# Tokens ordered by grid column, with branch B's softmax, copies and values cut to the 160 keys that a tile can see, in a two-layer encoder

## What is computed

```python
A  = differential attention (4 heads, T5 relative bias)
B  = 2-D neighbourhood attention on the 64-wide token grid (8 heads, own 2-D bias)
C  = dilated sliding-window attention (8 heads, T5 relative bias)
x += (sum_i sigmoid(g_i) * (branch_i @ W_br_i)) @ W_o
```

```python
kh = min(NA_ROWS_MAX, rows)          # 4, so every row
kw = min(NA_COLS, GRID_W)            # 16
cstart = jnp.clip(col - kw // 2, 0, GRID_W - kw)
cidx = cstart[:, None] + jnp.arange(kw)[None, :]
s = jnp.einsum('bhqd,bhrqcd->bhqrc', qrow, knb) + bias
pr = jax.nn.softmax(s.reshape(B, B_HEADS, GRID_W, kh * kw), axis=-1)
return jnp.einsum('bhqrc,bhrqcd->bhqd', pr, vnb)
```

## Time and profile before

| | |
|---|---|
| runs (us) | 1266.9, 1267.26, 1269.08 |
| profiled execution (us) | 1267.46 |
| its span, first to last instruction (us) | 1265.4 |
| granted TensorE clock, mean | 0.998 |
| TensorE matmul busy | 1255.7 us, 99% |
| VectorE busy | 842.6 us, 67% |
| ScalarE busy | 679.2 us, 54% |
| GpSimd busy | 39.0 us, 3% |
| DMA | 245.05 MB, mean 194 GB/s |

### The profile page before, as it was taken

The page is one execution under the profiler, slowest core; times in us unless marked ns, Lnnn a source line. Parts: engine busy times, 40 slices in busy tenths (PEclk is TensorE's granted clock), DMA queues, the critical chain, the costliest instruction groups (busy, mean ns, idle before and its releaser), DMA issues.

```text
span 1265.4 us, 17533 instructions
## 1 busy us (share of the span) xinstructions
PE 1255.7 (99%) x6763; PEld 1067.9 (84%) x6763; DVE 842.6 (67%) x1196; ACT 679.2 (54%) x920; POOL 39.0 (3%) x55
## 2 busy tenths in 40 slices
PE   9999999999999999999999999999999999999997
PEld 6888888888878888888888888888888788888886
DVE  6576667557767766556675666766577777655665
ACT  7454555546866354454554445554477543644544
POOL 0311100000000000000000000000000000000000
PEclk9999999999999999999999999999999999999999
DMA  8697855565644545555445555455556454555551
GB/s 281 233 288 233 262 215 200 199 213 187 238 124 148 190 171 195 199 188 182 178 184 199 199 183 185 163 204 201 194 203 214 122 192 169 188 194 199 199 192 40
DMA packets 59211, 245.05 MB, mean 194 GB/s; under 512 B 21344, under 2 KB 27616, under 8 KB 32408
## 3 DMA queue, kind: packets, MB, share of 16 engines
q1 hardware_dynamic: 58144, 242.54, 55.1%
q10 hardware_dynamic: 984, 1.80, 0.4%
q0 software_dynamic: 32, 0.02, 0.0%
HBM read 239.07 MB, written 5.27 MB: 193 GB/s over the span
## 4 chain that ended last, share of the span: by engine, by line
PE 97%; DVE 2%; issue 0%; DMA 0%; ACT 0%; POOL 0%; POOLq 0%; SPq 0%; DVEq 0%; ACTq 0%
PE bank L796 30%; PE bank L800 16%; PE bank L763 16%; PE bank L765 15%; PE bank L764 15%; PE bank L1117 1%; PE bank L1094 1%; PE bank L849 1%; PE bank L856 1%; PE bank L1108 1%; DMA params<-in_params 0%; DVE wlo L1227 0%; DVE nat L1483 0%; DVE qkT L1434 0%; DVE nat L1479 0%
## 5 line engine op out<-in xcount | busy, mean ns | idle before, releaser
L1227 DVE TENSOR_TENSOR wlo<-raw,whi 128x2048 fp32r<-128x2048 f32 x209 | 479.3, 2296 | 302.6 <-ACT whi L467 296.1
L467 ACT ACTIVATE whi<-raw 128x2048 fp32r<-128x2048 f32 x206 | 393.0, 1911 | 233.8 <-PE bank L800 143.5
L796 PE MATMUL bank<-xT,whi 128*128 128x512 f32 x1664 | 395.3, 390 | 0.0
L796 PEld LDWEIGHTS bank<-xT,whi 128*128 128x128 f32 x1664 | 308.7, 188 | 61.7
L800 PEld LDWEIGHTS bank<-xT,wlo 128*128 128x128 f32 x1664 | 207.1, 192 | 4.8 <-issue 0.5
L800 PE MATMUL bank<-xT,wlo 128*128 128x256 f32 x1664 | 209.2, 283 | 0.0
L763 PE MATMUL bank<-whi,xT 128*128 128x512 f32 x432 | 171.9, 398 | 1.0 <-DVE qkT L1434 1.0
L765 PE MATMUL bank<-whi,xT 128*128 128x512 f32 x432 | 168.5, 390 | 0.0
L764 PE MATMUL bank<-wlo,xT 128*128 128x512 f32 x432 | 168.3, 390 | 0.0
L763 PE MATMUL bank<-whi,hTh 128*128 128x512 f32 x320 | 124.5, 389 | 0.0
L764 PE MATMUL bank<-wlo,hTh 128*128 128x512 f32 x320 | 124.5, 389 | 0.0
(11 more groups left out here) (182 smaller groups left out, 1054.9 us busy)
## 6 DMA issues: line engine op xcount, KB each, us to landing
raw<-in_stream SPq DMA_DIRECT2D x209, 1024.0 KB, 4.8
bias<-t_rows SPq DMA_DIRECT2D x24, 256.0 KB, 8.2
bias<-in_rpb SPq DMA_DIRECT2D x16, 256.0 KB, 7.8
masked<-bias SPq DMA_DIRECT2D x8, 512.0 KB, 6.8
bias<-masked SPq DMA_DIRECT2D x8, 512.0 KB, 6.6
raw<-in_stream SPq DMA_DIRECT2D x10, 256.0 KB, 6.5
x<-in_x SPq DMA_DIRECT2D x4, 256.0 KB, 5.6
raw<-in_stream ACTq DMA_DIRECT2D x2, 256.0 KB, 4.4
```

Of the source, the lines that this page charges most:

```text
L467: act.activation(whi[:, s, :], raw[:, s, :], ACT.Copy).then_inc(hi_ready, 1)
L796: return pe.matmul(dst[blk][:, :], whi[:, s, w], xT[:, 4 * a + k, :, :].rearrange("p a s -> p (a s)"), start=start, stop=stop)
L1227: dve.tensor_tensor(wlo[:, s, :], raw[:, s, :], whi[:, s, :].bitcast(F32), ALU.subtract).then_inc(unit_split, 1)
```

## The change

Tokens lie by grid column: partition p of tile t holds grid column 32 t + p // 4 and grid row p % 4. x is loaded and the output stored through a rearranged view of DRAM (`rows_by_cols`). A tile of 32 columns sees at most 40 columns, so of the 256 keys it sees 160: keys 0 to 159 for tile 0 and 96 to 255 for tile 1 (`seen`). For branch B the bias step, the exponentials, the normalisation, the copy of the turned probabilities and the value matmuls work on those 160; the other 96 probabilities are filled with zeros before the turn, which is still in full width, as are the scores. The biases stay in order of position within a row of keys, and the bias step reads them with (column, row) strides, neighbours 64 elements apart (`rearrange("p (r c) -> p c r")`), for all three branches. The masked bias has a row per token, so each is stored in four DMAs of 64 partitions, one per grid row; each bias load of branches A and C becomes one per tile. Last, in VectorE's loop, the first reading of an odd unit's branch product stands ahead of the first due weight split and the second normalisation.

```diff
+COLS = GRID_W // TILES
+SEEN = (COLS + NA_COLS // 2) * GRID_H
+UNSEEN = S - SEEN
...
+        def rows_by_cols(ap, t, c0, c1):
+            return ap[0, :, c0:c1].rearrange("(r c) d -> c r d", r=GRID_H)[t * COLS:(t + 1) * COLS, :, :]
+        def by_cols(ap):
+            return ap.rearrange("p (c r) -> p c r", r=GRID_H)
+        def seen(b, t):
+            return slice(0, S) if b != BB else slice(0, SEEN) if t == 0 else slice(UNSEEN, S)
+        def seen_reversed(b, t):
+            return slice(0, S) if b != BB else slice(UNSEEN, S) if t == 0 else slice(0, SEEN)
...
-                sp.dma_start(masked[j, :, :], bias[:, j % 2, :, :, :].rearrange("p m t k -> p (m t k)")).then_inc(masked_stored, 16)
+                for r in range(GRID_H):
+                    half = slice(r % 2 * GRID_W, (r % 2 + 1) * GRID_W)
+                    sp.dma_start(masked[j, r::GRID_H, :].rearrange("c (m k) -> c m k", m=2), bias[half, j % 2, :, r // 2, :]).then_inc(masked_stored, 16)
...
-                    src = bass.AP(t5_rows.tensor, head * 512, [[1, P], [P, TILES], [1, S]])
-                    sp.dma_start(bias[:, ring, m, :, :], src).then_inc(bias_landed[ring], 16)
+                    for t in range(TILES):
+                        src = bass.AP(t5_rows.tensor, head * 512 + t * COLS, [[1, COLS], [GRID_W, GRID_H], [1, S]])
+                        sp.dma_start(bias[:, ring, m, t, :], src).then_inc(bias_landed[ring], 16)
...
-                        e = act.activation(probs_of(s)[:, m, t, ::-1], sneg_of[s % 2][:, m, t, :], ACT.Exp, scale=-1.0,
+                        p_seen = probs_of(s)[:, m, t, seen(s // 4, t)]
+                        e = act.activation(p_seen[:, ::-1], sneg_of[s % 2][:, m, t, seen_reversed(s // 4, t)], ACT.Exp, scale=-1.0,
...
-                                last = pe.matmul(o_turns(b, blk // 2)[DH * m:DH * m + DH, blk % 2, :], v[:, b, kb, d0:d0 + DH],
-                                                 pT_of[s % 2][:, m, kb, :], start=kb == 0, stop=kb == 1)
+                                asking = seen(b, kb)
+                                last = pe.matmul(o_turns(b, blk // 2)[DH * m:DH * m + DH, blk % 2, asking], v[:, b, kb, d0:d0 + DH],
+                                                 pT_of[s % 2][:, m, kb, asking], start=kb == 0, stop=kb == 1, skip_group_check=b == BB)
...
-                            r = dve.tensor_tensor_reduce(out=sneg_of[ring][:, m, t, :], in0=pair_bank(s, m)[:, t * S:(t + 1) * S],
-                                                         in1=bias[:, ring, 0 if b == BA else m, t, :], scale=-1.0, scalar=3e38,
+                            keys = seen_reversed(b, t)
+                            added = bias[:, ring, 0 if b == BA else m, t, :] if b != BB else bias[:, ring, t, m, :]
+                            r = dve.tensor_tensor_reduce(out=by_cols(sneg_of[ring][:, m, t, keys]),
+                                                         in0=by_cols(pair_bank(s, m)[:, t * S + keys.start:t * S + keys.stop]),
+                                                         in1=added.rearrange("p (r c) -> p c r", r=GRID_H)[:, keys.start // GRID_H:keys.stop // GRID_H, :],
+                                                         scale=-1.0, scalar=3e38,
...
+                        if s // 4 == BB:
+                            dve.memset(pr[:, :, 0, SEEN:S], 0.0)
+                            dve.memset(pr[:, :, 1, 0:UNSEEN], 0.0)
...
                     if j < PAIRS:
                         normalize(j)
+                    _, b, n, _ = MIX[j + 1]
+                    branch_now = MIX[j + 1][0] == "br"
+                    if branch_now:
+                        branch_tile(b, n, U_MIX + j + 1, 0)
                     for w in due[:1]:
                         to_lo(l, w)
                     if j < PAIRS:
                         normalize(j + 1)
                     split_o(j)
-                    _, b, n, _ = MIX[j + 1]
-                    branch_now = MIX[j + 1][0] == "br"
-                    if branch_now:
-                        branch_tile(b, n, U_MIX + j + 1, 0)
```

More of the change, by code:

```diff
@@ L55 @@
 RPB_ROWS, RPB_PITCH = TILES * GRID_H, 128
+COLS = GRID_W // TILES
+SEEN = (COLS + NA_COLS // 2) * GRID_H
+UNSEEN = S - SEEN
+assert NA_ROWS >= GRID_H and COLS * GRID_H == P
 MASK_AT = [6 + 3 * j for j in range(DEPTH * BLK + 1)]
@@ L163, in build @@
         t5_rows = nc.dram_tensor("t5_rows", [T5_HEADS, 512], F32, kind="Internal").ap()
-        masked = nc.dram_tensor("masked", [DEPTH * BLK, P, 2 * TILES * S], F32, kind="Internal").ap()
+        masked = nc.dram_tensor("masked", [DEPTH * BLK, S, 2 * S], F32, kind="Internal").ap()
         t5_high, t5_split, early_mean = map(sem, ("t5_high", "t5_split", "early_mean"))
@@ L240, in n_bias @@
         def n_bias(l, s):
-            per = {BC: 2, BB: 1, BA: 1}
+            per = {BC: 2 * TILES, BB: 1, BA: TILES}
             return 16 * DEPTH * BLK + l * (16 * sum(per[q // 4] for q in range(s % 2, PAIRS, 2))) + 16 * sum(per[q // 4] for q in range(s % 2, s + 1, 2))
@@ L272, in probs_of, with seen_by_keys @@
             return home
+        def rows_by_cols(ap, t, c0, c1):
[6 more added lines that the diff above has]
+            return slice(0, S) if b != BB else slice(UNSEEN, S) if t == 0 else slice(0, SEEN)
+        def seen_by_keys(ap):
+            return bass.AP(ap.tensor, ap.offset, [list(ap.ap[0]), [S + UNSEEN, TILES], [1, SEEN]])
         def pair_bank(s, m):
@@ L300, in load_unmasked @@
                 if j >= 2:
-                    sp.wait_ge(masked_stored, 16 * (j - 1))
+                    sp.wait_ge(masked_stored, 16 * GRID_H * (j - 1))
                 for half in range(2):
@@ L317, in load_bias @@
                 if b == BB:
-                    sp.dma_start(bias[:, ring, :, :, :].rearrange("p m t k -> p (m t k)"), masked[l * BLK + blk, :, :]).then_inc(bias_landed[ring], 16)
+                    sp.dma_start(bias[:, ring, :, :, :].rearrange("p t m k -> p t (m k)"),
+                                 masked[l * BLK + blk, :, :].rearrange("(t p) k -> p t k", p=P)).then_inc(bias_landed[ring], 16)
                     return
@@ L331, in load_x @@
             def load_x(t, n):
-                sp.dma_start(x[:, t, n * 512:(n + 1) * 512], x_in[0, t * P:(t + 1) * P, n * 512:(n + 1) * 512]).then_inc(x_landed[2 * n + t], 16)
+                sp.dma_start(x[:, t, n * 512:(n + 1) * 512], rows_by_cols(x_in, t, n * 512, (n + 1) * 512)).then_inc(x_landed[2 * n + t], 16)
             load_x(0, 0)
@@ L354, in _ @@
                 sp.wait_ge(t5_stored, 16)
-                sp.wait_ge(masked_stored, 16 * DEPTH * BLK)
+                sp.wait_ge(masked_stored, 16 * GRID_H * DEPTH * BLK)
                 load_bias(l, 0)
@@ L368, in _ @@
             sp.wait_ge(out0_ready, 1)
-            sp.dma_start(out[0, 0:P, :], nat[:, 0:2, :].rearrange("p a b -> p (a b)")).then_inc(out_stored, 16)
+            sp.dma_start(rows_by_cols(out, 0, 0, D), nat[:, 0:2, :].rearrange("p a b -> p (a b)")).then_inc(out_stored, 16)
             sp.wait_ge(out1_late, 1)
-            sp.dma_start(out[0, P:S, 512:D], nat[:, 3, :]).then_inc(out_stored, 16)
+            sp.dma_start(rows_by_cols(out, 1, 512, D), nat[:, 3, :]).then_inc(out_stored, 16)
             sp.wait_ge(out_stored, 48)
@@ L623, in copy_turned @@
                     act.wait_ge(probs_turned, n_probs_turned(l, s, m))
-                    act.activation(pTa_of(s) if s // 4 == BA else pT_of[s % 2][:, m, :, :],
-                                   pair_bank(s, m)[:, :].rearrange("p (a b) -> p a b", a=2), ACT.Copy).then_inc(pT_copied, 1)
+                    dst, src = pTa_of(s) if s // 4 == BA else pT_of[s % 2][:, m, :, :], pair_bank(s, m)[:, :].rearrange("p (a b) -> p a b", a=2)
+                    if s // 4 == BB:
+                        dst, src = seen_by_keys(dst), seen_by_keys(src)
+                    act.activation(dst, src, ACT.Copy).then_inc(pT_copied, 1)
             def o_to_hi(l, b, half):
@@ L755, in _ @@
             act.wait_ge(out1_early, 1)
-            act.dma_start(out[0, P:S, 0:512], nat[:, 2, :]).then_inc(out_stored, 16)
+            act.dma_start(rows_by_cols(out, 1, 0, 512), nat[:, 2, :]).then_inc(out_stored, 16)
         @block.tensor
@@ L1471, in normalize @@
                     if s < 8:
+                        if s // 4 == BB:
+                            dve.memset(pr[:, :, 0, SEEN:S], 0.0)
+                            dve.memset(pr[:, :, 1, 0:UNSEEN], 0.0)
                         for m in range(2):
                             for t in range(TILES):
-                                w = dve.tensor_scalar(pr[:, m, t, :], pr[:, m, t, :], r[:, m, t:t + 1], None, ALU.mult)
+                                part = pr[:, m, t, seen(s // 4, t)]
+                                w = dve.tensor_scalar(part, part, r[:, m, t:t + 1], None, ALU.mult)
                             w.then_inc(normed, 1)
```

## The result

The changed kernel takes 1271.24 us (median of 8 runs, 1269.41 to 1273.7) against 1267.29 (8 runs): ratio 1.0028, interval 1.002 to 1.0037. The prediction was 1264.1, faster; its range ended at 1267.1. The profiled execution took 1270.0 us, span 1267.9, 2.5 us over the span before.

A forecast was written before the change was run, and what follows sets the result against it. TensorE, busy 1255.7 of 1265.4 us, was taken to bound the kernel. Terms -2.5 - 1.4 + 0.5 + 0.2 = -3.2 us gave 1264.26, or 1264.1 against the median; range 1262.4 to 1267.1.

The forecast's parts named there:

- (b): Mixer unit 10: moving VectorE's read of unit 9's first half removes TensorE's wait, -1.4 us for two layers; ends 0 and -1.4.
- (d): Strided bias read in VectorE's score steps: +0.26 us an instruction, mostly inside margins, +0.2 us in all; ends 0 and +1.9.
- (a): Branch B's value matmuls, 160 columns instead of 256: 0.079 us less per step, 32 steps, -2.5 us; ends 0 and -3.4.
- the first rival: Branch B's value step keeps its 0.217 us because bringing in values as weights sets it: 1266.6 us, chance 0.10.
- (c): First feed-forward block: the masked bias stored in four pieces delays weight unit 10's load, +0.5 us once; ends 0 and +1.1.
- At nothing: Changes priced at zero, among them 24 more bias loads on SyncE, delaying a weight load 1.5 us without harm.
- The slower rival: Strided read is dear: 0.80 us an instruction eats the gain at units 4, 9, 12; 1274 at 0.94 us; chance 0.09.

The follow-up runs named there:

- the undone edit: Changed kernel with biases early and stores late, branch B's value matmuls and copy of turned probabilities put back to full width: 1266.49 us, against 1263.8 without that.

## Why the prediction was wrong

The forecast was -3.2 us, the profile has +2.5. Of these 5.7 us, 4.3 are unit 12 of the mixer, 1.1 the store and 0.7 the output; (b) and (d) give 0.2 each back.

- **(a) right.** 2.5 us forecast, 2.5 in the trace by stages, 2.7 by the undone edit. Columns set the value step; the first rival is out.
- **(b) right for its wait, wrong for what stands behind it.** The stops went, worth 1.6 us (forecast 1.4). The step that failed is the sentence that "TensorE asks for both only after all of unit 10". It asked who waits for the split of unit 11 and answered with TensorE alone. SyncE waits for it too, before it issues the load of unit 13, and behind that stand the biases of pairs 10 and 11.
- **(c) mechanism right, size wrong.** I multiplied the 0.37 us of one store by three. A piece held the queue for 0.64, four for 2.57, and the load came 2.0 us later instead of 1.1: +1.6 instead of +0.5, outside the ends that I gave. By the Trainium skill (SBUF — State Buffer, section on the DMA port swizzle) I had an estimate of +1.6 and kept it out of the sum. The trace agrees with its rule for 64 partitions: the four pieces moved at about 200 GB/s. That the estimate gave the same number is luck in part: 128 partitions took back only 0.8 of the 2.2 us of the queue, and in other executions the wait was up to 3.0.
- **(d) right per instruction (+0.19 against +0.26 us), wrong in its margins.** At unit 12 I took 2.45 us, from VectorE's idle time ahead of one split. That margin holds only while the biases land on time, and pair 11's did not have any: its step started at 379.01, the moment of landing. The chain that ended there began at pairs 8 and 9, eight slow steps and the moved read ahead of a split. This chain is what the sum lacked: waits of 1.7 and 1.9 us at unit 12, 4.3 us with what follows them, where (d) had +0.2. The gains of (a) and (b) took the rest: TensorE came to unit 12 earlier, VectorE later. A margin measured before is spent from both sides.
- **"At nothing", the bias loads.** I asked which weight load they delay, at 0.37 us an issue (it took 0.6), and not when they themselves land. Their doubling did no harm, their place in the queue did.
- **The slower rival** had the right place (unit 12) by the wrong mechanism: it needed an instruction of 0.80 us, and 0.61 was enough. The Trainium skill's rule on lines of 16 bytes (Advanced Engine Details and Errata, SBUF Cachelines) points the right way: 64 elements apart costs 0.19 us in 256, 2 elements apart nothing. Whether the lines are the cause is not shown, since the short runs changed with the distance.
- **The output** costs 0.7 us, not some tenths.

Without the late biases and the store 1263.8 was measured; the sum without (c) is 1263.6. That they lie so close is luck in part: the output's 0.7 is in no term, and (b), 0.2 better, and (d), at nothing, make up for 0.4 of it.

## What to carry to other kernels

When work is moved on an engine, list everything that waits for each instruction behind it, DMA queues included, and follow each queue to the next compute instruction; a queue in order turns a late split into a late bias. Read a margin at the operand that lands last, and spend it from both sides: the waiting engine comes earlier by every gain ahead of it. Where a DMA is cut into pieces, price a piece by a row of its own shape, or take the longer hold as the term.

## What the runs showed that I had not expected

- Behind waits of 1.8 to 3.0 us TensorE ran at 1.2 GHz for the next eight matmuls or so (granted clock 0.51, +1.6 us), behind the longest for more, in some executions only; behind a wait of 2.6 us, in the profile with early biases, it did not.
- A store of the same 128 KB holds SyncE's queue for 0.43 us from 128 partitions, for 0.61 from 64 (medians); the output store, same bytes in another order of rows, for 0.61 instead of 0.34.
- The store whose outermost dimension was 2 moved at up to 51 GB/s, where the same bytes in the other cuts moved at about 200 GB/s or more.
